# A one-core hybrid block: gathering the experts' output rows in two passes

## The reference

```
h = rms_norm(x1, norm2_g) * (1 + sc2) + sh2
g_idx = top 1 of softmax(h @ w_rg + b_rg) over 4 groups; e_idx = top 2 of 8 experts in it
y[token] = sum over its 2 experts of weight * ((silu(gate) * up) @ w_e_out[e]),
           gate, up = split(h @ w_e_in[e])
out = x1 + gt2 * y
```

## Time and profile before

| What | us |
|---|---|
| Median of 3 runs | 1766.65 (1766.56 to 1767.51) |
| Profiled execution, its own time | 1765.35 |
| Its span | 1763.6 |
| TensorE, VectorE, ScalarE, POOL busy | 1646.5, 1110.1, 537.9, 372.6 |
| Last matmul starts in the piece at | 1714.51 |
| First late instruction of POOL (line 906) | 1725.73 |

### The profile page before, as it was taken

The page is one execution under the profiler, slowest core; times in us unless marked ns, Lnnn a source line. Parts: engine busy times, 40 slices in busy tenths (PEclk is TensorE's granted clock), DMA queues, the critical chain, the costliest instruction groups (busy, mean ns, idle before and its releaser), DMA issues.

```text
span 1763.6 us, 36677 instructions
## 1 busy us (share of the span) xinstructions
PE 1646.5 (93%) x15177; PEld 980.8 (56%) x15177; DVE 1110.1 (63%) x2641; ACT 537.9 (31%) x1235; POOL 372.6 (21%) x471
## 2 busy tenths in 40 slices
PE   5999999999999899999999999986999999999990
PEld 3455444454444677777677645554566566665560
DVE  2486616655776455666665635564887878887754
ACT  5221323433443223333323321113333333332310
POOL 3030000000223564455664350110000000000003
PEclk9999999999999999999999999997999999999995
DMA  9377219100222422142122187568999999999998
GB/s 350 124 247 274 72 51 324 35 25 24 84 84 96 145 63 58 43 141 67 43 64 60 63 270 276 203 238 347 405 423 424 423 423 423 425 423 423 425 378 307
DMA packets 137720, 386.77 MB, mean 219 GB/s; under 512 B 13914, under 2 KB 83464, under 8 KB 124300
## 3 DMA queue, kind: packets, MB, share of 16 engines
q1 hardware_dynamic: 113744, 304.72, 45.5%
q10 hardware_dynamic: 15708, 50.54, 7.6%
q0 software_dynamic: 8112, 29.23, 4.5%
HBM read 331.10 MB, written 66.08 MB: 225 GB/s over the span
## 4 chain that ended last, share of the span: by engine, by line
PE 76%; DMA 9%; DVE 8%; SPq 3%; issue 2%; ACT 1%; POOL 1%; ACTq 0%; POOLq 0%; DVEq 0%
PE bank L342 75%; DMA arena<-in_w_e_in 5%; SPq L466 2%; DVE arena L2645 1%; DMA arena<-in_w_ada 1%; DVE arena L2635 1%; DMA arena<-y_slots,ints 1%; PE bank L1092 1%; DMA arena<-in_w_in 1%; DVE arena L2373 0%; POOL arena L906 0%; PE bank L1412 0%; DVE arena L2076 0%; DMA arena<-token_blocks 0%; DVE arena L2324 0%
## 5 line engine op out<-in xcount | busy, mean ns | idle before, releaser
L342 PE MATMUL bank<-arena 128*32 128x256 f32 (+11 forms) x14798 | 1603.6, 381 | 43.6 <-issue 4.1
L342 PEld LDWEIGHTS bank<-arena 128*32 128x32 f32 (+4 forms) x14798 | 934.9, 133 | 686.4 <-issue 433.7
L1917 ACT ACTIVATE arena<-arena 128x96 f32<-128x96 f32 (+1 forms) x372 | 151.8, 497 | 219.9 <-DVE arena L2635 219.9
L2635 DVE STREAM_TRANSPOSE arena<-arena 32x192 f32<-32x192 f32 x496 | 183.6, 370 | 6.5 <-ACT arena L1908 0.2
L2645 DVE STREAM_TRANSPOSE arena<-arena 32x128 f32<-32x128 f32 x384 | 158.4, 412 | 4.8
L906 POOL DMA_INDIRECT arena<-y_slots,ints x16 | 16.4, 1023 | 537.0 <-DMA y_slots<-arena 531.1
L826 POOL TENSOR_TENSOR arena<-arena 64x256 f32<-64x256 f32 x96 | 70.2, 731 | 59.3 <-DVE arena L2343 52.5
L2618 DVE TENSOR_TENSOR arena<-arena,bank 128x128 f32<-128x128 f32 x96 | 21.9, 283 | 92.8 <-ACT arena L1926 92.3
L2367 DVE TENSOR_TENSOR arena<-arena,bank 128x128 f32<-128x128 f32 (+1 forms) x40 | 11.3, 283 | 74.2 <-PE bank L342 74.2
L1926 ACT ACTIVATE arena<-bank 128x128 f32<-128x128 f32 x96 | 19.6, 276 | 111.2 <-PE bank L342 111.2
L2076 DVE RECIPROCAL arena<-arena 128x512 f32<-128x512 f32 x10 | 33.5, 3349 | 30.1 <-ACT arena L1620 30.1
(11 more groups left out here) (356 smaller groups left out, 1335.5 us busy)
## 6 DMA issues: line engine op xcount, KB each, us to landing
arena<-in_w_e_in SPq DMA_DIRECT2D x64, 2048.0 KB, 26.2
arena<-in_w_e_out SPq DMA_DIRECT2D x32, 2048.0 KB, 28.2
arena<-in_w_ada SPq DMA_DIRECT2D x12, 2048.0 KB, 12.8
arena<-in_w_in SPq DMA_DIRECT2D x48, 512.0 KB, 4.3
arena<-x_slots ACTq DMA_DIRECT2D x31, 384.0 KB, 11.1
y_slots<-arena ACTq DMA_DIRECT2D x32, 288.0 KB, 14.6
y_slots<-arena POOLq DMA_DIRECT2D x21, 384.0 KB, 18.2
arena<-in_w_in SPq DMA_DIRECT2D x3, 2048.0 KB, 21.7
```

Of the source, the lines that this page charges most:

```text
L342: return nc.tensor.matmul(o, l, r, start=start, stop=stop)
L1917: ins = A.activation(e_xT[s][:, k, QT * w:QT * (w + n)].rearrange("p (w m) -> p w m", m=QT), raw_columns(c, k % 2, w, n), ACT.Identity, sc ...
L2635: ins = V.transpose(e_raw[ts(b, QT), :, ts(g, QT)], pieces[:, :, b, :])
```

## The change

The gathers of y rows become two passes over the 8 tiles.

- **Early pass** (POOL). It waits for the stores of experts 0 to 28 (`EARLY` = 29) and for y of expert 29, then issues the 12 gathers of tiles 0 to 5; after y of expert 30 it issues the 4 of tiles 6 and 7. They use `i_s1` and `i_s2` with a bound of `EARLY * CAP - 1`, so rows of experts 29 to 31 lie outside and are dropped.
- **Late pass** (POOL, at the place of the old gathers). 16 gathers with new indices `i_l1`, `i_l2`, in which every slot below `EARLY * CAP` has 8192 added, so that only rows of experts 29 to 31 (and extra blocks) lie inside the bound. Before each pair of tiles it waits for that pair's early gathers.
- **Buffers and semaphores.** Each tile has its own pair `f_y`: tiles 0 to 5 in the place of set 2, tiles 6 and 7 in columns 0 to 4096 of set 0. `f_x` moves to columns 4096 to 12288 of set 0. Tiles share semaphores as `FY` says: 0 and 1, 2 and 3, 4 and 5, then 6 and 7 alone. VectorE waits for all gathers of a pair before its first tile. The waits of POOL for `f_sum` are gone.
- **x rows** (SP). The 8 loads wait for y of expert 30 and for the early gathers of tiles 4 and 5.
- **Extra blocks** load their weights into set 1, and `x_hot` and its like move.

```diff
+        EARLY = NE - 3
+        FY = (0, 0, 1, 1, 2, 2, 3, 4)
-        f_x = [view(24576 + 1024 * t, D) for t in range(NT)]
-        f_y = [[view(2048 * i, D), view(2048 * i + 1024, D)] for i in range(4)]
+        f_x = [view(4096 + 1024 * t, D) for t in range(NT)]
+        f_y = [[view((24576 if t < 6 else -12288) + 2048 * t + 1024 * k, D) for k in range(TOPK)] for t in range(NT)]
...
-            sp.wait_ge(sem("y"), 2 * (NE - 2))
+            sp.wait_ge(sem("y"), 2 * (NE - 1))
+            sp.wait_ge(fy_in[2][0], fy_in[2][1] + 64)
             for t in range(NT):
                 sp.dma_start(f_x[t], x1_t[t]).then_inc(sem("gate_in"), 16)
...
             n_extra = pool.value_load(i_ex[0:1, NX:NX + 1], min_val=0, max_val=NX)
+            pool.wait_ge(sem("y_st0"), 32 * ((EARLY + 1) // 2))
+            pool.wait_ge(sem("y_st1"), 32 * (EARLY // 2))
+            for t in range(NT):
+                if t in (0, 6):
+                    pool.wait_ge(sem("y"), 2 * (NE - 2) + (2 if t else 0))
+                for k, ix in enumerate((i_s1, i_s2)):
+                    pool.indirect_dma_start(out=f_y[t][k], out_offset=None, in_=yslot_d[0:EARLY * CAP],
+                                            in_offset=bass.IndirectOffsetOnAxis(ap=ix[:, t:t + 1], axis=0),
+                                            bounds_check=EARLY * CAP - 1, oob_is_err=False)\
+                        .then_inc(fy_in[FY[t]][0], 16)
             pool.wait_ge(sem("xs_used"), NE)
...
             for t in range(NT):
-                if t >= 4:
-                    pool.wait_ge(sem("f_sum"), t - 3)
-                for k, ix in enumerate((i_s1, i_s2)):
-                    pool.indirect_dma_start(out=f_y[t % 4][k], out_offset=None, in_=yslot_d,
-                                            in_offset=bass.IndirectOffsetOnAxis(ap=ix[:, t:t + 1], axis=0))\
-                        .then_inc(fy_in[t % 4][0], 16)
+                if t % 2 == 0 or t == NT - 1:
+                    pool.wait_ge(fy_in[FY[t]][0], fy_in[FY[t]][1] + 32 * FY.count(FY[t]))
+                for k, ix in enumerate((i_l1, i_l2)):
+                    pool.indirect_dma_start(out=f_y[t][k], out_offset=None, in_=yslot_d,
+                                            in_offset=bass.IndirectOffsetOnAxis(ap=ix[:, t:t + 1], axis=0),
+                                            bounds_check=NB * CAP - 1, oob_is_err=False)\
+                        .then_inc(fy_in[FY[t]][0], 16)
...
+                link(TS(r_over, r_div, float(EARLY * CAP), float(8 * T), ALU.is_lt, ALU.mult))
+                link(TT(r_over, r_over, r_div, ALU.add))
+                for a, isl in enumerate((i_l1, i_l2)):
+                    V.tensor_copy(isl, r_over[:, :, a])
...
             for t in range(NT):
-                y0, y1 = f_y[t % 4]
-                dve.wait_ge(fy_in[t % 4][0], fy_in[t % 4][1] + 32 * (t // 4) + 32)
+                y0, y1 = f_y[t]
+                dve.wait_ge(fy_in[FY[t]][0], fy_in[FY[t]][1] + 64 * FY.count(FY[t]))
```

More of the change, by code:

```diff
@@ L302, in hybrid_block @@
         r_ex, r_exs = rtmp(NX, NE), rtmp(NX + 1)
-        x_hot, x_in = view(32768, NT, P), view(33792, NT, NX)
+        x_hot, x_in = view(12288, NT, P), view(13312, NT, NX)
         def rank_bank(t):
             return PS[6][:, 64:64 + NE] if t < NT - 2 else PS[4 * (t - NT + 2)][:, 0:NE]
-        x_hot2, x_in2 = view(34304, NT, P), view(35328, NT, NX)
+        x_hot2, x_in2 = view(13824, NT, P), view(14848, NT, NX)
         sb_i = ctx.enter_context(nc.sbuf_tensor("ints", [P, 160], i32))[:, :]
         i_tok, i_s1, i_s2 = (sb_i[:, 8 * k:8 * k + 8] for k in range(3))
+        i_l1, i_l2 = sb_i[:, 124:132], sb_i[:, 132:140]
         i_tab = sb_i[:, 40:40 + NBP]
@@ L391, in hybrid_block @@
         s_slot = [sem("weights_slot0"), sem("weights_slot1")]
-        fy_in = [(sem("fy_in0"), 0), (sem("fy_in1"), 0), (sem("x_sc0"), 16 * NT), (sem("x_sc1"), 16 * NT)]
+        fy_in = [(sem("fy_in0"), 0), (sem("fy_in1"), 0), (sem("x_sc0"), 16 * NT), (sem("x_sc1"), 16 * NT), (sem("slots_zero"), 16 * NX + 128)]
         m_in = [(sem("wide_in0"), 80), (sem("wide_in1"), 80), (s_slot[0], slot_target[2]), (s_slot[1], slot_target[3])]
@@ L626, in _ @@
             with sp.If(n_extra > 0):
+                sp.wait_ge(sem("router_dve"), X_TABLE)
                 with sp.Fori(0, NX) as j:
@@ L631, in _ @@
                         for k in range(2):
-                            sp.dma_start(WE[0][k], I["w_e_in"][0, ds(e, 1), 512 * k:512 * k + 512, :]
+                            sp.dma_start(WE[1][k], I["w_e_in"][0, ds(e, 1), 512 * k:512 * k + 512, :]
                                          .rearrange("a (p k) n -> p (a k) n", p=P)).then_inc(sem("extra_w"), 16)
-                        sp.dma_start(WE[0][2], I["w_e_out"][0, ds(e, 1)]
+                        sp.dma_start(WE[1][2], I["w_e_out"][0, ds(e, 1)]
                                      .rearrange("a (p k) n -> p (a k) n", p=P)).then_inc(sem("extra_w"), 16)
@@ L1542, in _ @@
                         pe.wait_ge(sem("e_act"), NE + j)
-                        first(1, WE[0], 0)
-                        first(1, WE[0], 1).then_inc(sem("win_used"), 1)
+                        first(1, WE[1], 0)
+                        first(1, WE[1], 1).then_inc(sem("win_used"), 1)
                         pe.wait_ge(sem("e_hT"), NE + j + 1)
                         pe.wait_ge(sem("y_out"), 2 * (NE + j))
-                        second(WE[0])
+                        second(WE[1])
                     with pe.Else():
```

## The result

The changed kernel takes 1783.16 us (median of 4 runs, 1779.9 to 1784.98), the kernel before beside it 1766.61 (4 runs, 1763.13 to 1767.51): ratio 1.0095, 95% interval 1.0075 to 1.0115. It is slower by 16.6 us; 4.6 were forecast. The profiled execution took 1779.9, the shortest of the four; its span is 1778.0 against 1763.6, so these profiles have 14.4 us to explain.

A forecast was written before the change was run, and what follows sets the result against it. The tail was taken as bound by DMA bytes, the changed one by late x rows: landed 1744.0, plus 21.1 us of sums and 3.1, span 1768.2 against 1763.6, +4.6 us, time 1771.2, range 1762.5 to 1775.

The forecast's parts named there:

- Early gathers from 1698.0, one in 1.27: POOL's early pass: starts at 1698.0, one gather in 1.27 us, the twelfth issued at 1712.0.
- What they do to the last weights: 1.3 us on close(31): Expert 31's weights give way to early gathers and land at 1715.8, so close(31) starts 1.3 us later.
- The rival that gathers go ahead of weights: Last weights: w_e_out of 31 lands at 1726, PE ends at 1731.5, time 1773.3 us; chance 0.13.
- Stores of 31 two later: Expert 31's stores among two other queues: 2 us added to 4.04, bounds 0 and 9; landed at 1728.2.
- Dropped rows cost no bytes: Gathers of both passes: rows outside the bound are assumed to move no bytes and add no POOL fee.
- The fifth rival: Dropped rows cost as much as kept ones: first sum 1752.7, time 1779.9 us; chance 0.05.
- SP goes on at 1727.4, x rows landed at 1744.0: SP waits for the twelfth early gather until 1727.4; its eight x row loads then land at 1744.0.
- The forecast's path: Before the first sum: x rows, landed at 1744.0, end the wait, 7 us behind the first pair's gathers (1737.1).
- Sums without a gap, 21.1 us, and 3.1 to the end: Tail: VectorE's sums run 21.1 us from 1744.0 to 1765.1, then 3.1 us to the span's end, 1768.2.
- the forecast's own sign (over 0.5): Tail: the forecast is wrong if gaps of over 0.5 us stand between sums.
- Signs: Late-half DMA near 1.0 from 1698 to 1743, close(31) about 1716, first sum 1742 to 1746 waiting for x.
- 6.6 us of 7.1: Tail: 8.4 MB less lets sums run without gaps, 7.1 us less with the first sum where it is.

The follow-up runs named there:

- e2: Changed kernel with the early pass using the late indices, so every row is dropped and nearly no bytes move: 1778.54 us (before: 1766.11).
- e3: Changed kernel with the early gathers replaced by plain 512 KB loads of contiguous rows, still issued by POOL on its software queue: 1774.82 us (before: 1766.11).
- e4: Changed kernel with the early gathers replaced by plain 512 KB loads issued by SP on its own hardware queue: 1771.51 us (before: 1766.11).
- e10: Changed kernel with early gathers of as many 1 KB pieces instead of 4 KB rows: 1764.23 us (before: 1766.14).
- e14: Changed kernel with early gathers of as many 2 KB pieces instead of 4 KB rows: 1762.82 us (before: 1767.29).
- e15: Changed kernel with some 3 us of other POOL work after each pair of the first 12 early gathers: 1777.62 us (before: 1767.29).
- e6: Kernel before plus 6 POOL gathers of 1 KB pieces into free space, at the early pass's place: 1770.54 us (before: 1767.96).
- e7: Kernel before plus 6 POOL gathers of 1 KB pieces, with 3 us of memsets after each pair: 1770.17 us (before: 1767.96).
- e5: Kernel before plus 12 POOL gathers of 1 KB pieces into free space, at the early pass's place: 1771.36 us (before: 1767.96).
- e9: Kernel before plus 4 POOL gathers of whole 4 KB rows, x rows loaded where they were: 1769.96 us (before: 1766.14).
- e12: Kernel before plus 12 POOL gathers of 1 KB pieces, with SP's x rows waiting for y of expert 30: 1768.1 us (before: 1766.14).
- e13: Kernel before plus 4 POOL gathers of whole 4 KB rows, with x rows waiting for y of expert 30: 1769.69 us (before: 1767.29).
- e17: Changed kernel with one short POOL write of zeros after each of the first six pairs of early gathers: 1770.92 us, ratio 1.0023.
- e1: Changed kernel with all 16 early gathers waiting for y of expert 30 instead of 29: 1783.67 us (before: 1766.11).
- e18: Changed kernel with one short POOL write of zeros after the 4th, 8th and 12th early gather: 1772.01 us, ratio 1.0026.

## Why the prediction was wrong

- *Early gathers from 1698.0, one in 1.27.* Right: 1698.47, one in 1.30.
- ***What they do to the last weights: 1.3 us on close(31).* This step failed.** It looked for the price of the gathers in the weights' transfers alone and took it for granted that TensorE's own pace in step(31) is untouched. There the runs show 14.0 us, and 1.7 more in close(31) at the lower clock. The rival that gathers go ahead of weights had a late TensorE too (1731.5), by weights landing late; e2, with no bytes, and e3 and e4, with all of them, show that it is not that. Clear of this effect close(31) starts at 1714.68 (e4) and 1714.64 (e10), the old 1714.51, and at 1718.28 in e3, where it waits 1.55 for w_e_out. But e3 is 2.6 us behind before its first load (expert 29 stored at 1699.54 instead of 1696.94). Counted from that store, close(31) starts after 17.6 us before, in e4, e14 and e15, 17.7 in e10 and 18.7 in e3: the weights' delay itself is 0 to 1.2, so this term alone was sized well. Why the gathers slow TensorE stays open (below).
- *Stores of 31 two later.* The sign was right, the size not: 5.2, within the stated bounds of 0 and 9. With TensorE in time it is 0 to 4: first store to late pass takes 5.3 us in e6, 7.3 in e7, 8.0 in e14 and 8.5 to 9.3 in e5, e9, e10, e12 and e13, against 5.3.
- *Dropped rows cost no bytes.* Right (29.24 MB in q0). That they cost nothing at all was too much: each is still a packet, and e2, with nothing but such rows in its early pass, slows TensorE as much. The fifth rival, that they cost bytes, names 1752.7 for the first sum and 1779.9, close to 1753.39 and 1783.16; that is chance, for its bytes are not there.
- *SP goes on at 1727.4, x rows landed at 1744.0.* The issue came at 1725.98, and q1 moved x rows to 1747, 21 us instead of 16.6. In the changed kernel the late pass, not the x rows, ended the wait for the first sum, 1753.39. The forecast's path, in which the x rows end that wait, is the one of e17 (issued 1730.20, first sum 1746.63, so 16.4 us later) and of e3 (17.0). That e4's time is 1771.51, the forecast's, is in part luck: its late pass starts at 1736.23 and not 1729.1, its x rows are issued 2.8 us later, and late gathers, not x rows, end its wait for the first sum.
- *Sums without a gap, 21.1 us, and 3.1 to the end.* Near: 21.6 and 3.1, but with a gap of 1.24 us, which by the forecast's own sign (over 0.5) counts against it; a tile takes 2.52 us when nothing holds it, not 2.64, and the two differences cancel.
- *Signs.* The DMA engines were not busy to 1743: from 1720 to 1725 their share was 0.31. Close(31) started at 1728.38 and not near 1716, and the first sum lies outside 1742 to 1746 and waits for y rows.

**What stays open** is through what the gathers hold TensorE. Shown: it comes with indirect gathers of 4 KB rows (the changed kernel, e1, e2, e17, e18) and not with as many of narrower pieces (e10, e14), it wants several one behind the other (not e15), and it is neither bytes (e2), nor full DMA engines (e2 from 1710), nor POOL's issuing of DMAs as such (e3). It is not the packets alone either: e3 has as many, of 4 KB and on the same queue, twelve loads in 6.5 us, and loses nothing. And e13 has four wide gathers at the same time and pace as e18's first four, with 100 matmuls from 1700 to 1705 where e18 has 61. The two differ in the buffers and semaphores, in half of the indices and in the kernel around. That it is writing into these buffers is unlikely, for e2 writes next to nothing; the rest was not tried. The Trainium skill, "Runtime: NRT & Kernel Launch", section "Instruction fetch mechanics", says that an engine's sequencer fetches its program in blocks of 16 KiB by a DMA queue of its own. The trace agrees: its instruction queue moves 16 KB packets, 122 for 2.00 MB in both kernels. In the changed kernel one starts at 1702.66, takes 1.1 us, and the next comes at 1722.22, after 254 matmuls and weight loads; in the kernel before, the one at 1702.77 is followed by that at 1711.53, after 280. So none is under way from 1703.8 to 1715.7, while TensorE pauses, and their rarity there looks like a consequence of the slow pace and not its cause. "DMA: Bandwidth & Descriptors", section "SWDGE vs HWDGE vs iDMA", of the Trainium skill, says that POOL writes its DMAs' descriptors into rings in SBUF, for direct and indirect ones alike, and that those of SP never touch this path. That the path alone does it does not fit: e4, on SP's queue, is unharmed, but so is e3, which takes POOL's.

## What to carry to other kernels

Moving work to where an engine's queue is idle is not free because its bytes are: look whether the compute engine beside it keeps its pace, by counting its instructions in 5 us windows. Try the moved DMAs alone, but do not take a clean result for an acquittal: here they were harmless when added to the kernel before (e9, e13) and harmful in the changed one. Where the tail waits on a small store, what is put into the queues just before it can come back as that store's lateness, here by 0 to 5 us. The saving was real (6.6 us of 7.1); the lateness of the first sum, 21.1 us, was three times as much.

## What the runs showed of the hardware, unexpected

- A run of indirect gathers of 4 KB rows, one in 1.30 us, took TensorE from 80 to 100 matmuls in 5 us to 12 to 17, with the clock at 1.00 at first and no wait named (changed kernel, e1, e2). As many gathers of 1 or 2 KB pieces (e10, e14), and plain loads (e3, e4), did nothing of it.
- Rows dropped by the bound are packets without bytes, and a gather that drops them all takes POOL as long (3.78 us busy from 1705 to 1710 in e2 and in e10, with its pieces of 1 KB).
- With q0 and q1 both full, the two stores of expert 30 (288 and 96 KB) took 8.9 and 10.7 us to land in the changed kernel; those of 31 before, with q1 at 16% of the engines beside them, 2.6 and 4.0. From 1735.9 to 1736.6 the three queues had 33, 34 and 34 packets, and the stores' were the small ones (0.04 MB).
- A gather of 128 rows is 144 packets at 4 KB (changed kernel), 80 at 2 KB (e14) and 48 at 1 KB (8880 packets in q0, e10).
